# Two-layer transformer trunk on one core: dummy products in two waits, a moved pair of column products, and weight copies on other engines

## The chip, the core and the metric

The kernel runs on one core of a Trainium2 chip. The core's engines are TensorE (PE in the rows, its weight loads PEld), VectorE (DVE), ScalarE (ACT), GpSimd (POOL) and SyncE (SP), which issues the DMAs. They run side by side and wait for each other on semaphores. The metric is the device time of one execution in microseconds (us).

## The reference, cut to what matters

```python
D_MODEL, SEQ, DEPTH = 1024, 1024, 2
def reference(x, c, w_ada, b_ada, g_pre, g_post, w_in, w_out, diff_lambda, diff_subln):
    cond = jax.nn.silu(c)
    for i in range(DEPTH):
        ada = cond @ w_ada[i] + b_ada[i]
        shift, scale, gate = jnp.split(ada[:, None, :], 3, axis=-1)
        h = rms_norm(x, g_pre[i]) * (1.0 + scale) + shift
        u = h @ w_in[i]
        mix_in, z = u[..., :3 * BRANCH_WIDTH], u[..., 3 * BRANCH_WIDTH:]
        if i % N_MIXERS == 0:
            y = stick_breaking_attention(mix_in)
        else:
            j = i // N_MIXERS
            y = diff_attention(mix_in, diff_lambda[j], diff_subln[j], diff_lambda_init(i))
        y = (y * jax.nn.silu(z)) @ w_out[i]
        x = x + gate * rms_norm(y, g_post[i])
    return x
```

mix_in holds q, k and v for 16 heads of 64. Everything is float32.

## The kernel before, in words

**Arithmetic.** A float32 product is made from two reduced-precision parts of each operand: "high" is a rounded copy, "low" is the rest. One tile of 128 rows of the sum costs three products of 128x512: high with high, high weights with low activations, low weights with high activations. So every operand has a high copy (mostly ScalarE's) and a low subtraction (VectorE's or GpSimd's) before TensorE can use it.

**Stages.** The preparation (class `Prologue`) normalises x, turns it (feature rows on partitions), computes shift and scale, and projects q, k and v of the first pair of heads. Then layer 0 runs eight pairs of heads; in each the attention of the pair stands between the projection products of this pair's z (the gate branch) and the next pair's q, k and v (L666). The last pair has no next one, and takes the first part of the output projection (L1134) instead. `project_out` does the rest and, after layer 0, the first pair of layer 1. Layer 1 has the same shape with differential attention. Each engine has one written-out program; nothing is reordered at run time.

**The preparation on TensorE.** `warm(n)` multiplies a bf16 tile of zeros, which nothing reads; `turn(t)` turns one of eight row tiles; `row(n, h)` multiplies the conditioning vector with a slice of w_ada; `columns(i)` brings shift and scale, which lie in a row (i even) or are still to be summed over partitions (i odd), into columns, with eight tiny matmuls (L529). After `columns(0)` and `columns(1)` VectorE makes the first half of the columns, and then for each unit (128 features by 512 tokens) ScalarE writes h_hi (L346) and VectorE h_lo (L447). `project(kinds, phase, ...)` is the projection (L544): phase 0 is features 0 to 511 by tokens 0 to 511, phase 1 the same features by tokens 512 to 1023, phase 2 features 512 to 1023, which need `columns(2)` and `columns(3)`. The kinds are 0 (q), 1 (k) and 2 (v). VectorE sums `columns(1)`'s operand with L418 to L424.

**After it.** ScalarE copies the q and k sums out of PSUM (L686), packs them per head (L747: q and two copies of k for each of two heads), copies v, and makes the high part of z's weights (`split_hi(act, 0, 3)`, L632). These weights are loaded into the slot that k's weights leave. VectorE packs the low parts (L756 to L762) and GpSimd makes the low part of z's weights (L638). Head 0 of a pair is used in steps 0 to 7 of 16, head 1 from step 8 on.

**The last pair of layer 1.** In step 2 TensorE multiplies the first of four token tiles with the output weights, feature row by feature row: of the eight rows w_out is cut into it uses 0 to 6, each as soon as its high copy stands (`weights_ready`). ScalarE makes the copies of rows 0 to 5 (L983), VectorE those of 6 and 7 (L989), GpSimd all eight low parts (L1001). Then comes token tile 1, which needs its own high and low activations (ScalarE L1048, VectorE L1056) and the PSUM bank, which ScalarE empties (L1141).

Of the kernel before, what the change touches and what calls it, by code (L numbers as in the profile page):

```python
# [29 lines left out]
KT = D // P  # L30
# [156 lines left out]
class Prologue:  # L187
# [6 lines left out]
    T = ((0, 1), (6, 7), (0, 1), (6, 7), (6, 7), (4, 1), (6, 7), (4, 1))  # L194
    WARM = (24, 12)
    ACC = ((3, 4), (0, 1), (6, 7))
# [295 lines left out]
    def tensor(self, pe):  # L492
        nc, m = self.nc, self.m
# [69 lines left out]
        turn(3)  # L563
        columns(0)
        columns(1)
        pe.wait_ge(self.left_kept, 4)
        pe.wait_ge(self.right_kept, 4)
# [7 lines left out]
        project((0, 1), 1, range(self.LOW))  # L575
        for phase in range(2):
            project((2,), phase, range(self.LOW))
        columns(2)
        columns(3)
        project((0, 1), 2, range(self.LOW))  # L580
        for kind in range(3):
# [331 lines left out]
class OutProjection:  # L913
# [5 lines left out]
    def __init__(self, nc, m, sb, layer, order, sems, before=None):  # L919
# [19 lines left out]
        if before:  # L939
            self.gate_stored, self.weights_in = before.gate_stored, before.weights_in  # L940
            self.weights_hi_done, self.weights_lo_done = before.weights_hi_done, before.weights_lo_done
            self.weights_hi_second_done = before.weights_hi_second_done
            self.hi_done, self.lo_done, self.product, self.kept = (before.hi_done, before.lo_done, before.product,
                                                                   before.kept)
            self.early_hi, self.early_lo = before.early_hi, before.early_lo
            self.early_product, self.early_kept = before.early_product, before.early_kept
            return

        def sem(name):
            return nc.alloc_semaphore(f"o_{name}")  # L950
# [3 lines left out]
        self.weights_hi_done, self.weights_lo_done = sem("w_hi_done"), sem("w_lo_done")  # L954
        self.weights_hi_second_done = sem("w_hi_second_done")

# [28 lines left out]

    def weights_hi_second(self, dve, k):

        dve.wait_ge(self.weights_in[k // 2], 16 * self.layer + 16)
        self.nc.vector.tensor_copy(self.m["wo_hi"][:, k, :], self.m["wo_raw"][:, k, :]  # L989
                                   ).then_inc(self.weights_hi_second_done, 1)  # L990

    def weights_ready(self, engine, k):

        if self.layer and k >= 6:
            engine.wait_ge(self.weights_hi_second_done, k - 5)
        else:
            engine.wait_ge(self.weights_hi_done, KT * self.layer + k + 1)

# [13 lines left out]
    EARLY = 2 * (2 * HI + 2 * (HI + LO))  # L1012
# [164 lines left out]
def stick_breaking(nc, m, pro, proj, outp, w_out, w_ada, x, gate_rows):  # L1177
# [69 lines left out]
    HI_OWN, HI_NEXT = {0: (4, 5)}, {8: 0, 11: 1, 12: 2, 15: 3}  # L1247
# [31 lines left out]
    pack = HeadPacking(nc, m, "s")  # L1279
# [32 lines left out]
    with nc.Block() as block:  # L1312
# [163 lines left out]
        def _(act):  # L1476
# [51 lines left out]
            def pack_hi(p, n):  # L1528
                if n in (0, 1):
                    act.wait_ge(proj.u_done, done(6 * p + 2 * n + 1))  # L1530
                if n == 0:
                    act.wait_ge(logits, done(NCH * (p - 1) + LOOP.at[TILES // 2] - 1))
                if n == 3:
                    act.wait_ge(logits, done(NCH * p - 1))
                pack.hi(act, n)
# [6 lines left out]
            def pair(p, first, project):  # L1542
                for s in range(TILES if project else STEPS):
# [17 lines left out]
                    for kind, half in U_AT[s] if project else ():  # L1561
                        keep_u(p + 1, kind, half)
                    for n in () if first else HI_OWN.get(s, ()):
                        pack_hi(p, n)
# [10 lines left out]
            for kind in range(2):  # L1575
                for half in range(2):
                    keep_u(0, kind, half, m["pm"][pro.ACC[kind][half]])
                for n in ((0,), (1, 2, 3, 4, 5))[kind]:
                    pack_hi(0, n)
            for half in range(2):  # L1580
                keep_u(0, 2, half)
            proj.split_hi(act, 0, 3)
            pair(0, True, True)
# [6 lines left out]
        def _(dve):  # L1590
# [93 lines left out]
            def pair(p, first, project):  # L1684
                for s in range(TILES if project else STEPS):
# [12 lines left out]
                    lo_own = LO_OWN if project else LAST_LO_AT  # L1698
                    if not first and s in lo_own:
                        pack.lo(dve, p, lo_own[s])  # L1700
# [17 lines left out]

            for n in range(4):
                pack.lo(dve, 0, n)  # L1720
            pair(0, True, True)
            with dve.Fori(1, PAIRS - 1) as p:
# [5 lines left out]
        def _(pool):  # L1728
# [17 lines left out]

            proj.split_lo(pool, 0, 3)
            pair(0, True)
# [4 lines left out]
def differential(nc, m, pro, proj, outp, w_out, first, source, gate_rows):  # L1753
# [37 lines left out]
    LAST_Z_AT = [[0, 1] if s == EARLY - 1 else [] for s in range(STEPS)]  # L1791
    OUT_HI_AT = {1: (0, 1, 2), 2: (3, 4, 5)}
    OUT_LO_AT = {2 + k // 2: (k, k + 1) for k in range(0, KT, 2)}
# [32 lines left out]
    with nc.Block() as block:  # L1826
# [112 lines left out]
        def _(act):  # L1939
# [78 lines left out]
            def pair(p, project):  # L2018
                for s in range(STEPS):
# [32 lines left out]
                    for k in () if project else OUT_HI_AT.get(s, ()):  # L2052
                        outp.weights_hi(act, k)
                    if s == EARLY and not project:
                        outp.early_split_hi(act, EARLY_AT[s], pack)
                    for t, h in early_kept:
# [18 lines left out]
        def _(dve):  # L2075
# [91 lines left out]
            def pair(p, project):  # L2167
                for s in range(STEPS):
# [24 lines left out]
                    if s == EARLY + 1 and not project:  # L2193
                        z_gate(p)
                    if s == EARLY and not project:
                        for k in (6, 7):
                            outp.weights_hi_second(dve, k)
                    if s in EARLY_AT and (s == EARLY or s > EARLY + 1) and not project:
# [384 lines left out]
```

## Time and profile before

| | |
|---|---|
| median of 3 runs | 1428.17 us (1428.1 to 1428.66) |
| the profiled execution's own time | 1429.55 us |
| its span on the core | 1427.8 us |
| TensorE busy (matmul) | 1366.0 us, 96% |
| VectorE, ScalarE, GpSimd busy | 1012.6, 905.2, 384.4 us |
| mean granted TensorE clock | 0.985 of full speed |

The span is the part of the execution in which the engines work; about 1.8 us lie around it. A granted clock of 1.00 is the upper level (2.4 GHz) and 0.50 the lower one (1.2 GHz). TensorE's busy time counts a slow product as busy, so a stretch at 0.50 looks full.

### The profile page before, as it was taken

To read this page: it belongs to the slowest core of one execution; us is meant where nothing else is said; L and a number is where in the kernel's file an instruction comes from. 1 tells how busy PE (TensorE), PEld (TensorE's weight loads), DVE (VectorE), ACT (ScalarE), POOL (GpSimd) and SP (SyncE) were. 2 spreads that over 40 slices of the span, in tenths; PEclk is the share of its full clock that TensorE was granted. 3 is DMA by queue.
4 is the path that set the end of the run, shared out by engine and by line. 5 is a ranking of instruction groups with operands and counts; after the bars stand their busy time and mean duration, and the time that the engine had idled before them with its cause. 6 is when DMAs were issued, how large, how long until landed. Compare 5 with 4: busy or idle time off the path is not lost. (4 is left out here: it accounts for less than half of the span.)

```text
span 1427.8 us, 23466 instructions
## 1 busy us (share of the span) xinstructions
PE 1366.0 (96%) x7206; PEld 1127.8 (79%) x7206; DVE 1012.6 (71%) x1868; ACT 905.2 (63%) x1778; POOL 384.4 (27%) x255
## 2 busy tenths in 40 slices
PE   6979999999999999998899899999999999998997
PEld 3568888888888888877778688888888888886776
DVE  4556889787878787889578675757575656566654
ACT  3546667666666666676356576867676767675742
POOL 2103434333433343344100122222222222226000
PEclk8889999999999999999999999999999999999999
DMA  9111212031212121231143111010111111103114
GB/s 341 61 37 52 67 39 81 22 87 30 73 44 73 44 67 46 71 132 46 52 150 101 30 31 39 25 39 29 29 29 29 29 29 29 44 15 118 45 62 146
DMA packets 88591, 89.90 MB, mean 63 GB/s; under 512 B 3065, under 2 KB 68834, under 8 KB 88546
## 3 DMA queue, kind: packets, MB, share of 16 engines
q1 hardware_dynamic: 88256, 89.15, 19.8%
q8 instruction: 25, 0.41, 0.1%
q10 hardware_dynamic: 290, 0.18, 0.1%
q14 instruction: 20, 0.16, 0.0%
HBM read 80.92 MB, written 8.40 MB: 63 GB/s over the span
## 5 line engine op out<-in xcount | busy, mean ns | idle before, releaser
L666 PE MATMUL bank<-h_hi,w_hi 128*128 128x512 f32 x928 | 377.4, 407 | 4.9 <-POOL w_lo L638 4.9
L666 PE MATMUL bank<-h_hi,w_lo 128*128 128x512 f32 x928 | 373.6, 403 | 0.0
L666 PE MATMUL bank<-h_lo,w_hi 128*128 128x512 f32 x928 | 371.2, 400 | 0.0
L1739 POOL TENSOR_TENSOR sa<-sa,keep 128x128 f32<-128x128 f32 (+7 forms) x128 | 223.9, 1749 | 388.4 <-DVE keep L1601 388.4
L666 PEld LDWEIGHTS bank<-h_hi,w_hi 128*128 128x128 f32 x928 | 176.4, 190 | 33.8 <-issue 6.5
L1601 DVE TENSOR_TENSOR_SCAN keep<-keep 128x128 f32<-128x128 f32 (+7 forms) x128 | 194.8, 1522 | 10.9 <-ACT keep L1490 10.9
L666 PEld LDWEIGHTS bank<-h_hi,w_lo 128*128 128x128 f32 x928 | 175.8, 189 | 32.1
L666 PEld LDWEIGHTS bank<-h_lo,w_hi 128*128 128x128 f32 x928 | 176.0, 190 | 29.0
L638 POOL TENSOR_TENSOR w_lo<-w_raw,w_hi 128x1024 fp32r<-128x1024 f32 x30 | 72.6, 2419 | 431.0 <-ACT w_hi L632 431.0
L1489 ACT ACTIVATE sa<-bank 128x512 f32<-128x512 f32 (+2 forms) x192 | 94.6, 492 | 73.6 <-PE bank L1373 44.1
L1502 ACT ACTIVATE wt_hi<-bank 128x512 fp32r<-128x512 f32 (+2 forms) x192 | 87.5, 490 | 54.8 <-PE bank L1389 50.8
L1610 DVE TENSOR_TENSOR wt_lo<-bank,wt_hi 128x512 fp32r<-128x512 f32 (+2 forms) x192 | 100.5, 550 | 25.5 <-ACT wt_hi L1502 23.5
L2105 DVE CUSTOM_DVE_ANT_0 b<-bank,bias 128x512 f32<-128x512 f32 (+2 forms) x96 | 51.0, 557 | 70.0 <-PE bank L1855 69.7
L1951 ACT ACTIVATE b<-b,stat 128x128 f32<-128x128 f32 (+3 forms) x64 | 49.7, 776 | 72.7 <-DVE stat L2114 44.3
L1490 ACT ACTIVATE keep<-bank 128x512 f32<-128x512 f32 (+2 forms) x192 | 95.4, 497 | 0.0
L2141 DVE TENSOR_TENSOR wt_lo<-bank,wt_hi 128x512 fp32r<-128x512 f32 (+2 forms) x96 | 50.5, 554 | 58.2 <-ACT wt_hi L1974 57.2
L1389 PE MATMUL bank<-ident,sa 128*128 128x128 f32 x576 | 85.3, 275 | 0.3 <-DVE v L1681 0.3
L1959 ACT ACTIVATE b<-b,stat 128x128 f32<-128x128 f32 (+3 forms) x64 | 49.5, 773 | 45.9 <-DVE stat L2125 45.8
L1407 PE MATMUL bank<-wt_hi,v 128*128 128x256 f32 x320 | 75.8, 272 | 1.0 <-DVE wt_lo L1610 1.0
L1854 PE MATMUL bank<-k_hi,q 128*128 128x512 f32 (+2 forms) x192 | 70.2, 366 | 6.3 <-DVE stat L2105 4.5
L1407 PE MATMUL bank<-wt_lo,v 128*128 128x256 f32 x320 | 74.7, 280 | 0.0
L1389 PEld LDWEIGHTS bank<-ident,sa 128*128 128x128 f32 x576 | 66.0, 140 | 9.6 <-DVE v L1681 1.3
(253 smaller groups left out, 2919.5 us busy)
## 6 DMA issues: line engine op xcount, KB each, us to landing
w_raw<-in_w_in_dram SPq DMA_DIRECT2D x62, 512.0 KB, 4.1
ada_slice<-in_w_ada_dram SPq DMA_DIRECT2D x64, 256.0 KB, 2.7
p_ada<-in_w_ada_dram SPq DMA_DIRECT2D x8, 1024.0 KB, 13.0
wo_raw<-in_w_out_dram SPq DMA_DIRECT2D x8, 1024.0 KB, 4.8
p_x<-in_x_dram SPq DMA_DIRECT2D x8, 512.0 KB, 7.9
o_x<-in_x_dram SPq DMA_DIRECT2D x8, 512.0 KB, 4.1
x_between<-o_res SPq DMA_DIRECT2D x8, 512.0 KB, 2.9
o_x<-x_between SPq DMA_DIRECT2D x8, 512.0 KB, 4.7
```

What stands on the lines that cost most here:

```text
L638: engine.tensor_tensor(self.m["w_lo"][s][:, :, :], self.m["w_raw"][s][:, :, :], self.m["w_hi"][s][:, :, :].bitcast(F32), ALU.subtract).the ...
L666: mm = nc.tensor.matmul(self.bank[half][:, :], w[:, k, :], h[:, k, half * HALF:(half + 1) * HALF], start=(i == 0), stop=(i == GROUP - 1))
L1389: mm = nc.tensor.transpose(T[b % 2][:, j * P:(j + 1) * P], a[:, at:at + P], m["ident"][:, :])
L1407: mm = nc.tensor.matmul(O[:, c0:GW], m["v"][h][:, j, :], w[:, j, c0:GW], start=(j == 0 and w is m["wt_hi"]), stop=(j == tiles - 1 and w is ...
L1489: nc.scalar.activation(m["sa"][ring(t)][:, at:at + w], L[ch % 3][:, 0:w], ACT.Sigmoid, scale=SCALE)
L1490: nc.scalar.activation(m["keep"][KEEP[t]][:, at:at + w], L[ch % 3][:, 0:w], ACT.Sigmoid, scale=-SCALE).then_inc(gates, 1)
L1502: nc.scalar.activation(dst, T[b % 2][:, 0:w].rearrange("p (j q) -> p j q", q=P), ACT.Copy).then_inc(hi_done, 1)
L1601: nc.vector.tensor_tensor_scan(keep, keep, keep, 1.0, ALU.mult, ALU.bypass).then_inc(scanned, 1)
L1610: nc.vector.tensor_tensor(m["wt_lo"][:, js, c0:c0 + P], T[b % 2][:, 0:w].rearrange("p (j q) -> p j q", q=P), m["wt_hi"][:, js, c0:c0 + P]. ...
L1739: nc.gpsimd.tensor_tensor(a[:, at:S], a[:, at:S], m["keep"][KEEP[t]][:, at + 1:S + 1], ALU.mult).then_inc(weighted, 1)
L1854: nc.tensor.matmul(bank[:, 0:w], qs, m["k_hi"][n][:, k0:k0 + w], start=True, stop=False)
L2105: nc.vector.tensor_tensor_reduce(out=x[:, at:at + w], in0=L[ch % 3][:, 0:w], in1=m["bias"][:, at:at + w], scale=1.0, scalar=-3e38, op0=ALU ...
```

## The change

1. Two calls of `warm` (20 and 6 products on zeros) stand before and after `columns(1)`.
2. `columns(2)` and `columns(3)` stand between the two phases of v's projection, no longer behind them.
3. For the first pair, ScalarE makes the high part of z's weights ahead of v's two copies and of the two packs of head 1's k; these packs move into step 0 of the pair. VectorE packs head 1's low parts in steps 0 and 1, as in the other pairs, and makes the low part of z's weights in GpSimd's place.
4. In the last pair of layer 1 ScalarE makes the high copies of rows 6 and 7 of w_out too; the high activations of token tile 1 stand behind row 3 and ahead of row 4.

```diff
@@ -192,7 +192,7 @@
-    WARM = (24, 12)
+    WARM = (24, 12, 20, 6)
@@ -562,7 +562,9 @@
         turn(3)
         columns(0)
+        warm(self.WARM[2])
         columns(1)
+        warm(self.WARM[3])
         pe.wait_ge(self.left_kept, 4)
         pe.wait_ge(self.right_kept, 4)
         project((0, 1), 0, range(self.LOW))
@@ -573,10 +575,10 @@
         project((0, 1), 1, range(self.LOW))
-        for phase in range(2):
-            project((2,), phase, range(self.LOW))
+        project((2,), 0, range(self.LOW))
         columns(2)
         columns(3)
+        project((2,), 1, range(self.LOW))
         project((0, 1), 2, range(self.LOW))
         for kind in range(3):
             project((kind,), 2, range(0 if kind == 2 else self.LOW, KT))
...
@@ -983,18 +983,9 @@
-    def weights_hi_second(self, dve, k):
-
-        dve.wait_ge(self.weights_in[k // 2], 16 * self.layer + 16)
-        self.nc.vector.tensor_copy(self.m["wo_hi"][:, k, :], self.m["wo_raw"][:, k, :]
-                                   ).then_inc(self.weights_hi_second_done, 1)
-
     def weights_ready(self, engine, k):
 
-        if self.layer and k >= 6:
-            engine.wait_ge(self.weights_hi_second_done, k - 5)
-        else:
-            engine.wait_ge(self.weights_hi_done, KT * self.layer + k + 1)
+        engine.wait_ge(self.weights_hi_done, KT * self.layer + k + 1)
 
@@ -1560,7 +1551,7 @@
-                    for n in () if first else HI_OWN.get(s, ()):
+                    for n in HI_OWN.get(s, ()):
                         pack_hi(p, n)
@@ -1575,11 +1566,11 @@
-                for n in ((0,), (1, 2, 3, 4, 5))[kind]:
+                for n in ((0,), (1, 2, 3))[kind]:
                     pack_hi(0, n)
+            proj.split_hi(act, 0, 3)
             for half in range(2):
                 keep_u(0, 2, half)
-            proj.split_hi(act, 0, 3)
             pair(0, True, True)
@@ -1696,7 +1687,7 @@
-                    if not first and s in lo_own:
+                    if s in lo_own:
                         pack.lo(dve, p, lo_own[s])
@@ -1716,8 +1707,9 @@
-            for n in range(4):
+            for n in range(2):
                 pack.lo(dve, 0, n)
+            proj.split_lo(nc.vector, 0, 3)
             pair(0, True, True)
@@ -1744,7 +1736,6 @@
-            proj.split_lo(pool, 0, 3)
             pair(0, True)
@@ -1789,7 +1780,7 @@
-    OUT_HI_AT = {1: (0, 1, 2), 2: (3, 4, 5)}
+    OUT_HI_AT = {1: (0, 1, 2), 2: (3, 4, 5, 6, 7)}
     OUT_LO_AT = {2 + k // 2: (k, k + 1) for k in range(0, KT, 2)}
     EARLY_AT = {1: 0, 2: 1, 3: 2, 6: 3}
     MULTIPLY = shares(outp.EARLY, [0] * 2 + [28, 28, 14, 14, 14, 28, 14])
@@ -2051,8 +2042,8 @@
                     for k in () if project else OUT_HI_AT.get(s, ()):
                         outp.weights_hi(act, k)
-                    if s == EARLY and not project:
-                        outp.early_split_hi(act, EARLY_AT[s], pack)
+                        if k == 3:
+                            outp.early_split_hi(act, EARLY_AT[s], pack)
                     for t, h in early_kept:
                         if s != EARLY + 1 or h == 1:
                             outp.early_keep(act, t, h)
@@ -2192,9 +2183,6 @@
-                    if s == EARLY and not project:
-                        for k in (6, 7):
-                            outp.weights_hi_second(dve, k)
                     if s in EARLY_AT and (s == EARLY or s > EARLY + 1) and not project:
                         outp.early_split_lo(dve, EARLY_AT[s], pack)
```

TensorE in the preparation, from the fourth row tile to the first projection product:

```order
 L501 MATMUL bank<-ident,p_x_119 128x128 x8
 L529 MATMUL bank<-ones,p_ada_row 128x1 x4
+L507 MATMUL bank<-p_warm 128x512 x20
 L529 MATMUL bank<-ones,p_acc_125 128x1 x4
+L507 MATMUL bank<-p_warm 128x512 x6
 L544 MATMUL bank<-h_hi,w_hi_55 128x512
 L544 MATMUL bank<-h_lo,w_hi_55 128x512
```

Twenty dummy products now stand between the two column groups and six behind them.

TensorE further on, between v's phase 0 and phase 1 (`p_v_hi`, `p_v_lo` are v's weights):

```order
 L544 MATMUL bank<-h_lo,p_v_hi 128x512
 L544 MATMUL bank<-h_hi,p_v_lo 128x512
+L529 MATMUL bank<-ones,p_ada_row 128x1 x4
+L529 MATMUL bank<-ones,p_acc_127 128x1 x4
 L544 MATMUL bank<-h_hi,p_v_hi 128x512
 L544 MATMUL bank<-h_lo,p_v_hi 128x512
```

TensorE a little later, at the end of v's phase 1 and the start of phase 2 (q's weights):

```order
 L544 MATMUL bank<-h_lo,p_v_hi 128x512
 L544 MATMUL bank<-h_hi,p_v_lo 128x512
-L529 MATMUL bank<-ones,p_ada_row 128x1 x4
-L529 MATMUL bank<-ones,p_acc_127 128x1 x4
 L544 MATMUL bank<-h_hi,w_hi_55 128x512
 L544 MATMUL bank<-h_lo,w_hi_55 128x512
```

The eight column matmuls (4 and 4 in the program) moved ahead of v's second twelve products.

ScalarE from the end of the preparation to pair 0 (`w_hi_56<-w_raw_58` is z's weights, `k_hi_74` head 1's k), before:

```order
L686 ACTIVATE uq<-bank 128x512 x2
L747 ACTIVATE q_71<-uq 64x1024
L686 ACTIVATE uk<-bank 128x512 x2
L747 ACTIVATE k_hi_73<-uk 64x1024 x2
L747 ACTIVATE q_72<-uq 64x1024
L747 ACTIVATE k_hi_74<-uk 64x1024 x2
L686 ACTIVATE uv<-bank 128x512 x2
L632 ACTIVATE w_hi_56<-w_raw_58 128x1024
L1489 ACTIVATE sa_84<-bank 128x128
L1490 ACTIVATE keep_88<-bank 128x128
```

and now:

```order
L688 ACTIVATE uq<-bank 128x512 x2
L749 ACTIVATE q_71<-uq 64x1024
L688 ACTIVATE uk<-bank 128x512 x2
L749 ACTIVATE k_hi_73<-uk 64x1024 x2
L749 ACTIVATE q_72<-uq 64x1024
L634 ACTIVATE w_hi_56<-w_raw_58 128x1024
L688 ACTIVATE uv<-bank 128x512 x2
L1480 ACTIVATE sa_84<-bank 128x128
L1481 ACTIVATE keep_88<-bank 128x128
L749 ACTIVATE k_hi_74<-uk 64x1024 x2
```

The z copy stands two groups earlier, and the head 1 packs have gone behind the first sigmoids.

ScalarE in step 2 of the last pair of layer 1, before:

```order
L1974 ACTIVATE wt_hi<-bank 128x128
L983 ACTIVATE wo_hi<-wo_raw 128x1024 x3
L1048 ACTIVATE o_ahead_hi_164<-y 128x896
L1141 ACTIVATE o_parked_159<-bank 128x512 x2
L1048 ACTIVATE o_ahead_hi_163<-y 128x896
```

and now:

```order
L1965 ACTIVATE wt_hi<-bank 128x128
L983 ACTIVATE wo_hi<-wo_raw 128x1024
L1039 ACTIVATE o_ahead_hi_164<-y 128x896
L983 ACTIVATE wo_hi<-wo_raw 128x1024 x4
L1132 ACTIVATE o_parked_159<-bank 128x512 x2
L1039 ACTIVATE o_ahead_hi_163<-y 128x896
```

Two more weight copies stand ahead of the parked sums (`o_parked_159`), and the activations of token tile 1 (`o_ahead_hi_164`) ahead of four of the copies instead of behind them all.

## Rows read from the trace of the kernel before

**Rows 1.** the page of the profile, its first line
```profile
span 1427.8 us, 23466 instructions
```

**Rows 2.** who waited for whom, TensorE, whole span: total, times, longest
```profile
PE bank L1134 <- DVE o_ahead_lo L1056: 8.1, 4, 4.3
```

**Rows 3.** busy time by stretch: PE, PEld, DVE, ACT, POOL, clock, DMA
```profile
22.40:25.80 3.40, 2.00 (x16) 1.67 (x15) 2.42 (x5) 2.28 (x4) 0.32 (x1) 1.00 1.08 368
25.80:39.40 13.60, 4.92 (x15) 4.26 (x16) 10.95 (x17) 5.62 (x8) 7.99 (x8) 0.50 1.06 378
73.60:80.40 6.80, 6.05 (x14) 4.79 (x15) 6.63 (x12) 4.74 (x7) 0.00 (x0) 0.50 0.00 0
105.00:240.00 135.00, 135.00 (x762) 113.34 (x760) 108.23 (x142) 88.90 (x185) 49.79 (x29) 1.00 0.19 56
1309.20:1316.00 6.80, 6.18 (x15) 4.82 (x16) 3.69 (x7) 1.43 (x3) 6.80 (x3) 0.50 0.00 0
```

**Rows 4.** timeline of TensorE, preparation: start, length, instruction, idle before
```profile
24.50 1.05 PE L529 MATMUL bank<-ones,p_ada_row 1*128 1x1 f32 x8 [1.15 <-ACT p_ada_row L336]
31.90 1.87 PE L529 MATMUL bank<-ones,p_acc 128*128 128x1 f32 x8 [6.35 <-DVE p_acc L424]
36.34 0.77 PE L544 MATMUL bank<-h_hi,w_hi 128*128 128x512 f32 x1 [2.58 <-DVE h_lo L447]
...
50.69 8.21 PE L512 MATMUL bank<-p_ada,cond_act 128*1 128x512 f32 x16
```

**Rows 5.** timeline of the weight loads, dummy products at the start
```profile
5.41 3.12 PEld L507 LDWEIGHTS bank<-p_warm 128*128 128x128 bf16 x15 [0.17 <-issue]
```

**Rows 6.** timeline of TensorE, end of the preparation
```profile
70.91 1.05 PE L529 MATMUL bank<-ones,p_acc 128*128 128x1 f32 x8
74.35 0.77 PE L544 MATMUL bank<-h_hi,w_hi 128*128 128x512 f32 x1 [2.38 <-DVE h_lo L447]
...
88.19 0.39 PE L544 MATMUL bank<-h_hi,p_v_hi 128*128 128x512 f32 x1
...
93.40 0.39 PE L544 MATMUL bank<-h_hi,p_v_lo 128*128 128x512 f32 x1
...
98.89 0.77 PE L666 MATMUL bank<-h_hi,w_hi 128*128 128x512 f32 x1 [4.86 <-POOL w_lo L638]
```

**Rows 7.** timelines of DVE, ACT and POOL there; the page's issues (last)
```profile
73.51 0.69 DVE L447 TENSOR_TENSOR h_lo<-p_h,h_hi 128x512 fp32r<-128x512 f32 x1 [0.37 <-ACT h_hi L346]
...
81.80 0.69 DVE L447 TENSOR_TENSOR h_lo<-p_h,h_hi 128x512 fp32r<-128x512 f32 x1
...
112.98 1.20 DVE L638 TENSOR_TENSOR w_lo<-w_raw,w_hi 128x1024 fp32r<-128x1024 f32 x1
...
89.02 2.14 ACT L747 ACTIVATE k_hi<-uk 64x1024 fp32r<-64x1024 f32 x2
...
95.25 1.06 ACT L632 ACTIVATE w_hi<-w_raw 128x1024 fp32r<-128x1024 f32 x1
...
96.46 2.34 POOL L638 TENSOR_TENSOR w_lo<-w_raw,w_hi 128x1024 fp32r<-128x1024 f32 x1 [37.33 <-ACT w_hi L632]
...
w_raw<-in_w_in_dram SPq DMA_DIRECT2D x62, 512.0 KB, 4.1
```

**Rows 8.** timelines of DVE, ACT and PE, last pair of layer 1
```profile
1293.54 1.08 DVE L1056 TENSOR_TENSOR o_ahead_lo<-y,o_ahead_hi 128x896 fp32r<-128x896 f32 x1
...
1301.13 5.50 DVE L989 CAST wo_hi<-wo_raw 128x1024 fp32r<-128x1024 f32 x2
1306.55 3.22 DVE L1056 TENSOR_TENSOR o_ahead_lo<-y,o_ahead_hi 128x896 fp32r<-128x896 f32 x1
...
1321.71 1.28 DVE L2156 SCALAR_TENSOR_TENSOR y<-y,lam,z_sig 128x1024 f32<-128x1024 f32 x1 [2.43 <-ACT z_sig L2001]
...
1299.84 2.94 ACT L983 ACTIVATE wo_hi<-wo_raw 128x1024 fp32r<-128x1024 f32 x3
...
1309.82 0.80 PE L1134 MATMUL bank<-wo_hi,o_ahead_hi 128*128 128x512 f32 x1 [4.27 <-DVE o_ahead_lo L1056]
```

More of the change, by code:

```diff
@@ L941, in __init__ @@
             self.weights_hi_done, self.weights_lo_done = before.weights_hi_done, before.weights_lo_done
-            self.weights_hi_second_done = before.weights_hi_second_done
             self.hi_done, self.lo_done, self.product, self.kept = (before.hi_done, before.lo_done, before.product,
@@ L954, in __init__ @@
         self.weights_hi_done, self.weights_lo_done = sem("w_hi_done"), sem("w_lo_done")
-        self.weights_hi_second_done = sem("w_hi_second_done")
         self.hi_done, self.lo_done = sem("hi_done"), sem("lo_done")
```

## The prediction

> **What bounds the kernel now.** I read the page first: a span of 1427.8 us [rows 1], in which TensorE is busy 96%. Then the table of busy time by stretch, for how full that really is. From 105 to 240 us, pair 0 and most of pair 1, TensorE is busy 135.00 of 135.00 us at the full clock [rows 3]: it is the bound, and whatever reaches it earlier at 105 us is kept to the end. So the question is what happens in the few places where it waits or runs at the lower clock. The list of waits names the largest, o_ahead_lo (L1056), 8.1 us in 4 waits, the longest 4.3 us [rows 2]; the timeline shows that this one stands in the last pair of layer 1. The other large ones are in the preparation: 6.35 us before the summed columns, 2.58 us before the first projection product [rows 4], 2.38 us behind `columns(3)`, 4.86 us for z's weights [rows 6]. Last, the granted clock. It is 0.50 from 25.8 to 39.4, from 73.6 to 80.4 and from 1309.2 to 1316.0 us [rows 3], and each of the waits for h_lo, for z's weights and for o_ahead_lo is followed by products at low clock. Their price: from 74.35 us [rows 6] to 80.40 us there are 14 products [rows 3], 6.05 / 14 = 0.432 us each; between 88.19 and 93.40 us there are 23 steps of 5.21 / 23 = 0.2265 us [rows 6]. A product at low clock costs 0.205 us more.
>
> **Part 1, the dummy products.** Dummies at full clock go at 3.12 / 15, some 0.21 us each [rows 5]; at low clock they can't be faster than 0.43. `columns(0)` ends at 25.55 us [rows 4] and the clock falls at 25.8, so the twenty start low. Both ends: all low 8.6 us, to 34.2 us; all fast 4.2 us, to 29.8. The summed columns are ready at 31.9 us [rows 4]. I take about half low (at the start of the kernel dummies ran at the fast spacing), an end near 31.7 us, nothing lost. `columns(1)` then runs at full clock, as `columns(0)` did: 1.05 instead of 1.87 us [rows 4], **0.8 us**. The ScalarE and VectorE work behind it starts 0.8 us earlier, up to the row products at 50.69 us [rows 4]. If the six dummies keep the clock for the first projection (36.34 us), some 7 products save 1.4 us, but TensorE only comes sooner to row tiles 4 to 7, which ScalarE is still scaling. I take nothing for it. The row products themselves take 8.21 us for 16 [rows 4]; part of them ran at low clock, and wholly at full clock they would be shorter, which I take as 1 us, for the range alone.
>
> **Part 2, columns between the halves of v.** The gap of 2.38 us [rows 6] is the way from `columns(3)` through VectorE's column sums, ScalarE's h_hi and VectorE's h_lo. Twelve v products, 12 x 0.2265 = 2.7 us, now lie in it: **2.4 us** gone. No gap, so no low clock: 14 x 0.205 = **2.9 us**. Given back: h_lo comes at VectorE's pace, 73.51 to 81.80 us in seven steps [rows 7], 1.18 us a unit. Phase 2 takes 6 products (1.36 us) for each of the first four units, but only 3 (0.68 us) for the last four. First unit ready at t, last at t + 8.3; TensorE would be at unit 8 at t + 0.4 + 5.4 + 2.0 = t + 7.8. It waits **-0.5 us**. The move needs the row kept and the sum ready 2.7 us sooner; `columns(3)` waited for nothing before it [rows 6], so both were there with room.
>
> **Part 3, z's weights.** The end of v and the first score come 0.8 + 2.4 + 2.9 - 0.5 = 5.6 us earlier: TensorE is ready for z at 98.89 - 4.86 - 5.6 = 88.4 us. The load is issued when k's sums are done, 88.19 - 5.6 = 82.6 us, and lands 4.1 us later [rows 7], 86.7. ScalarE has by then done q, k and three of the head packs (1.07 us each, [rows 7]), about 86.4, so the high copy runs 86.8 to 87.9 (1.06 us). Before it stood behind two more packs and v's copies, at 95.25. VectorE takes 1.20 us where GpSimd took 2.34 [rows 7]: ready at 89.1. TensorE waits 0.7 us instead of 4.86: **4.2 us**. The clock stays up: twelve products were low after 98.89, 12 x 0.205 = **2.4 us**. The packs moved into step 0 (2.1 us of ScalarE) and VectorE's three operations of head 1 (under 1.3 us each) hide under steps 0 to 7; head 1 is not touched before step 8. Without that cover they would cost 2.1 us. What is late next is the load itself: with any gain ahead of it, the chain load, copy, subtraction moves along.
>
> **Part 4, last pair of layer 1.** VectorE's two casts take 5.50 us, then o_ahead_lo 3.22 us [rows 8], both while GpSimd makes wo_lo; alone o_ahead_lo takes 1.08 us, and a copy on ScalarE 2.94 / 3 = 0.98 us [rows 8]. Now, from 1299.84 us on [rows 8] at 0.98 us a copy and as much for the activations, ScalarE finishes row 3 at 1300.8, the activations at 1301.8 and rows 4 to 7 at 1302.8, 1303.8, 1304.7 and 1305.7. o_ahead_lo starts at 1301.9 and ends by 1305.1 even at 3.22 us. Row 4 comes 1.0 us later than before; behind row 6 stand four products of tile 0 and two of the score (6 x 0.2265 = 1.4 us), so TensorE gets to tile 1 at 1306.1 and waits for ScalarE to empty the bank, which I put at 1306.25. It starts tile 1 there instead of at 1309.82: **3.6 us**, and 14 products at full clock save 14 x 0.205 = **2.9 us**. Against it: VectorE's next work now falls under GpSimd's wo_lo copies, which go on to about 1317 us. The gating y operation (1.28 us at 1321.71, [rows 8]) is on the path to the next scores and would start near 1315.4. At the ratio of [rows 8], 3.22 to 1.08, it loses up to 1.3 us until GpSimd stops: **-1.2 us**. Sum 5.3 us. The Trainium skill has the rule (GPSIMD Engine Reference, Specifications): GpSimd's memory interfaces are shared with VectorE, and VectorE instructions with two SBUF inputs contend. It gives no factor; the trace agrees.
>
> **Sum.** 0.8 + 2.4 + 2.9 - 0.5 + 4.2 + 2.4 + 5.3 = 17.5 us. The profiled execution took 1429.55 us, 1.4 above the median, so 1412.1 there and 1410.7 beside the median. I say 1411.
>
> **The rivals.**
>
> *A, the columns bring the clock down.* From 22.4 to 25.8 us TensorE was busy 2.00 of 3.40 us, half of it tiny column products, and the clock fell right behind it [rows 3]. The same eight tiny products now lie in the middle of v. If it falls there, some 8 to 16 products run low, +1.6 to +3.3 us (at 0.205), of which 0.5 is the wait for h_lo anyway: near 1412.5. For it: that row. Against it: dense products on both sides. The Trainium skill (TensorE: Matmul & The Clock Gate, What's actually happening) says the clock drops after an idle spell; by that rule this rival would cost nothing. The row shows a fall without one, so I keep it.
>
> *B, the clock turns out kinder.* The row products at full clock (1.0 us), the low stretch in layer 0's last pair, behind a 2.7 us wait, missed (0.7 to 1.4 us): 1408.5 to 1409.5. The same page says the point of the change varies from run to run; the earlier times differ by only 0.56 us, so little of that shows here.
>
> *C, the last pair gives little.* The chain of score, bias, exponential, z gate after 1316 us is VectorE's and ScalarE's, not TensorE's. If all of it slows by 3.22 / 1.08 under GpSimd, or TensorE's wait there grows and the clock falls in it (14 x 0.205 = 2.9 us), the 5.3 us shrink to 0 to 2.4: 1413.5 to 1416.
>
> *D, z's load doesn't come sooner.* If it is held by other transfers, up to the 4.2 us are lost: 1415. The DMA queues are empty before it in this stretch, so this is unlikely.
>
> *E, slower: the dummies leave the clock low.* If products on zeros didn't hold it and the preparation and pair 0 ran low from 25.8 us on, each us of it would cost 0.47 us. To eat 17.5 us it must last 37 us beyond today's low stretches; the longest now is 13.6 us [rows 3]. From there on it decides, at 1429 and more.
>
> **How the numbers follow.** The forecast, 1409.5 to 1412, 0.40. A 0.20, B 0.15, C 0.18, D 0.04, E and the unforeseen 0.03. The range takes the forecast, A, B and most of C: 1407.5 to 1415.5. What a measurement can tell from no change is about 0.2%, 2.9 us. All cases but E lie beyond it: faster 0.96, same 0.02, slower 0.02.
>
> **What would show it.** In the timeline after: `columns(1)` at 1.05 us with no gap of 6 us before it but dummies; ScalarE's first row tile scaled 0.8 us earlier; phase 2 starting near 71.2 us at spacing 0.2265; z's first product near 89.1 us behind a wait under 1.5 us; clock 1.00 over 73.6 to 80.4 and at z's start. In the last pair, counted from the high copy of row 3: row 4 two ScalarE operations later, tile 1 starting 5.4 us after it instead of 9, and no low stretch. I would be wrong if pair 0 showed TensorE waits that it doesn't have now, or if steps 3 and 4 of the last pair had new waits on VectorE of more than 3 us.

## The result and the profile after

The changed kernel takes 1417.46 us (median of 4 executions, 1414.61 to 1419.73), the kernel before 1428.41 us in the same batch: ratio 0.9922, interval 0.9910 to 0.9934. Five more executions in a later batch give a median of 1416.54 us (1415.22 to 1420.56), ratio 0.992 (0.9907 to 0.9934). It is faster, by 11 to 11.5 us. The forecast was 17.4 us (1411), and the range ended at 1415.5 us.

The profiled execution took 1418.14 us. The page's first line, and the windows (columns as in [rows 3]):

```profile
span 1416.4 us, 23517 instructions
```
```profile
25.80:39.40 13.60, 11.83 (x49) 6.47 (x49) 11.56 (x18) 6.30 (x10) 8.04 (x8) 0.87 1.06 379
87.30:90.70 3.40, 1.01 (x5) 0.86 (x6) 2.22 (x3) 3.38 (x6) 0.45 (x1) 1.00 0.68 204
90.70:94.10 3.40, 3.40 (x10) 2.66 (x9) 0.65 (x1) 1.08 (x2) 0.93 (x1) 0.50 0.08 27
797.30:800.70 3.40, 1.53 (x8) 1.32 (x9) 1.76 (x5) 0.99 (x3) 0.00 (x0) 1.00 0.51 142
800.70:804.10 3.40, 3.40 (x11) 2.75 (x10) 0.00 (x0) 0.11 (x2) 0.00 (x0) 0.50 0.05 14
1309.30:1312.70 3.40, 1.46 (x12) 1.46 (x13) 3.29 (x14) 1.64 (x3) 0.00 (x0) 1.00 0.00 0
1312.70:1316.10 3.40, 3.40 (x11) 2.65 (x9) 1.56 (x5) 1.85 (x5) 0.00 (x0) 0.50 0.00 0
```

The long low stretch of the preparation has shrunk, the one at 73.6 us is gone. One at 636.8 us is the same as in the kernel before (647.0). Three more stand at 90.7, 800.7 and 1312.7 us, each right behind a stretch in which TensorE was busy 1.0 to 1.5 of 3.40 us.

TensorE in the preparation, to be laid beside [rows 4] and [rows 6]:

```profile
25.75 5.95 PE L507 MATMUL bank<-p_warm 128*128 128x512 bf16 x19 [0.16 <-issue]
31.94 1.05 PE L529 MATMUL bank<-ones,p_acc 128*128 128x1 f32 x8 [0.24 <-DVE p_acc L424]
...
35.84 0.47 PE L544 MATMUL bank<-h_hi,w_hi 128*128 128x512 f32 x1 [1.53 <-DVE h_lo L447]
...
43.19 1.09 PE L501 MATMUL bank<-ident,p_x 128*128 128x128 f32 x8 [1.63 <-ACT p_x L326]
...
49.72 7.03 PE L512 MATMUL bank<-p_ada,cond_act 128*1 128x512 f32 x16
...
77.81 0.47 PE L544 MATMUL bank<-h_hi,w_hi 128*128 128x512 f32 x1 [0.25 <-DVE h_lo L447]
...
86.75 0.22 PE L1363 MATMUL bank<-k_hi,q 128*128 128x128 f32 x1
...
89.69 0.47 PE L668 MATMUL bank<-h_hi,w_hi 128*128 128x512 f32 x1 [2.54 <-DVE w_lo L640]
```

The wait of 2.38 us behind `columns(3)` [rows 6] is gone; in its place TensorE waits 0.25 us for VectorE near the end of phase 2, at 77.81 us. The same product of z that stood at 98.89 us [rows 6] starts at 89.69, behind a wait of 2.54 us where 0.7 was forecast. What fed it, on ScalarE and VectorE, and the DMA queues from 84 to 88 us (queue, kind: packets, MB, share of the engines):

```profile
84.31 1.06 ACT L749 ACTIVATE q<-uq 64x1024 fp32r<-64x1024 f32 x1
87.28 1.06 ACT L634 ACTIVATE w_hi<-w_raw 128x1024 fp32r<-128x1024 f32 x1 [1.91 <-DMA w_raw<-in_w_in_dram]
...
88.37 1.22 DVE L640 TENSOR_TENSOR w_lo<-w_raw,w_hi 128x1024 fp32r<-128x1024 f32 x1 [3.20 <-ACT w_hi L634]
```
```profile
q1 hardware_dynamic: 562, 0.28, 23.4%
q8 instruction: 1, 0.02, 1.6%
```

ScalarE was free at 85.4 us and waited 1.91 us for the load. In the records 15 of the load's 16 completions have come by 85.5 us and the last at 87.26. There is one packet of queue 8, kind "instruction", 16384 bytes, from 85.21 to 86.20 us; while it runs the load starts no packet, and its last three start from 86.19 us on. The records don't say which DMA engine a packet ran on; that these three stood behind the large one on the same engine is inferred from these times.

The last pair of layer 1, to be laid beside [rows 8], ScalarE, VectorE, TensorE, GpSimd:

```profile
1291.87 1.04 ACT L983 ACTIVATE wo_hi<-wo_raw 128x1024 fp32r<-128x1024 f32 x1
1292.81 0.94 ACT L1039 ACTIVATE o_ahead_hi<-y 128x896 fp32r<-128x896 f32 x1
1293.65 3.89 ACT L983 ACTIVATE wo_hi<-wo_raw 128x1024 fp32r<-128x1024 f32 x4
...
1293.79 2.45 DVE L1047 TENSOR_TENSOR o_ahead_lo<-y,o_ahead_hi 128x896 fp32r<-128x896 f32 x1 [0.54 <-ACT o_ahead_hi L1039]
...
1307.14 3.05 DVE L2147 SCALAR_TENSOR_TENSOR y<-y,lam,z_sig 128x1024 f32<-128x1024 f32 x1 [2.30 <-ACT z_sig L1992]
...
1298.17 0.47 PE L1125 MATMUL bank<-wo_hi,o_ahead_hi 128*128 128x512 f32 x1
...
1311.24 0.33 PE L1845 MATMUL bank<-k_hi,q 128*128 128x128 f32 x1 [3.04 <-DVE stat L2096]
...
1288.02 21.09 POOL L992 TENSOR_TENSOR wo_lo<-wo_raw,wo_hi 128x1024 fp32r<-128x1024 f32 x8 [10.55 <-ACT wo_hi L983]
```

The order of the copies does what was forecast: token tile 1 starts without a wait, 5.3 us after row 3's copy ends. But z's gate on VectorE (L2147) takes 3.05 us under GpSimd's low copies, which run to 1309.1, where it took 1.28 in [rows 8]; TensorE waits 3.04 us for what follows it, and then comes the low stretch at 1312.7.

Last, two places that the forecast did not touch, both of the changed kernel: VectorE in layer 0's last pair, and TensorE at layer 1's first score.

```profile
635.05 0.75 DVE L1635 SCALAR_TENSOR_TENSOR ada_acc<-ada_slice,cond_act,ada_acc 128x512 f32<-128x512 f32 x1 [1.04 <-DMA ada_slice<-in_w_ada_dram]
```
```profile
799.17 0.32 PE L1845 MATMUL bank<-k_hi,q 128*128 128x128 f32 x1 [1.88 <-DVE q L886]
```

The kernel before waits 1.84 us at that score too, and there its clock stayed up.

The slice of w_ada at 635.05 us came late as z's load did: 15 of its 16 completions by 633.61 us, the last at 635.03, and a packet of queue 8 from 631.73 to 632.71. What it costs is seen in TensorE's wait for the o_ahead_lo behind it, here in the changed kernel and in the same kernel without part 1 (told below):

```profile
636.91 0.77 PE L1125 MATMUL bank<-wo_hi,o_ahead_hi 128*128 128x512 f32 x1 [3.29 <-DVE o_ahead_lo L1047]
...
633.73 0.47 PE L1123 MATMUL bank<-wo_hi,o_ahead_hi 128*128 128x512 f32 x1 [2.71 <-DVE o_ahead_lo L1045]
```

**Where the 11.4 us of the two profiled executions are**, from the starts of the same products in both traces (the sum of the columns is ready within 0.04 us in both, so the two can be laid over each other):

| place | forecast | seen |
|---|---|---|
| turn of token tile 4: 43.70 to 43.19 | 0.8 | 0.5 |
| to the end of the row products: 50.69 + 8.21 to 49.72 + 7.03 | 0 | 1.6 |
| to the first score: 93.63 to 86.75 | 4.8 | 4.7 |
| z's weights and the clock behind them, 6.88 to 10.12 | 6.6 | 3.2 |
| layer 0's last pair | 0 | -0.6 |
| layer 1's first score, the new low stretch | 0 | -1.65 |
| layer 1's last pair | 5.3 | 3.4 |

Small drifts between these places make up the rest.

### The profile page after: what moved, and what is told of

The parts are those of the page before. It is cut to its first block and busy times, and to the rows that moved or that the text cites. A ratio compares the mean times of both kernels' runs of the same rounds, so it can differ in the third digit from the quotient of the medians.

```text
span 1416.4 us, 23517 instructions
## 1 busy us (share of the span) xinstructions
PE 1365.8 (96%) x7231; PEld 1125.7 (79%) x7232; DVE 1008.6 (71%) x1867; ACT 907.4 (64%) x1780; POOL 382.8 (27%) x254
```

## The experiments

Every kernel was timed beside the kernel before (medians of 1427.8 to 1428.7 us). Executions of one kernel lie up to 5.3 us apart, so medians are compared with the changed kernel's nine executions, median 1416.8 us, and the traces by the starts of the same products. The first four each take one part out. Two theories were formed on the result. F puts the missing gain into fixed places: z's load late, z's gate slowed by GpSimd's copies, a low stretch more behind each. P says that every term holds and only the places of the clock's changes cost it.

**Part 1 out.**
```diff
-        warm(self.WARM[2])
         columns(1)
-        warm(self.WARM[3])
```


> The changed kernel without its 26 dummy products, all else as changed. Two theories of the missing 6 us (17.5 forecast, 11.4 seen in the traces). Theory F (fixed places): the terms of the record hold except at z's weights (the load landed 1.8 us late, the clock fell once more) and in the last pair (z gate slowed by GpSimd, clock fell), and the rest is where the clock happened to fall. Theory P (position only): all terms hold and only the position of the clock's changes cost 6 us. For this kernel both expect columns(1) at 1.87 us again (+0.8) and the row products at 8.2 instead of 7.0 us (+1.2): 2.0 us slower than the changed kernel, give or take one low stretch (1.6 us). If the record's 0.8 alone were right: +0.8.

Measured 1415.75 us (1413.31 to 1417.28), ratio 0.9913 (0.9899 to 0.9926): 1.0 us under the changed kernel, where both theories had it 2.0 us slower. Its trace, TensorE:

```profile
32.27 1.86 PE L529 MATMUL bank<-ones,p_acc 128*128 128x1 f32 x8 [6.34 <-DVE p_acc L424]
...
44.07 1.09 PE L501 MATMUL bank<-ident,p_x 128*128 128x128 f32 x8
...
50.60 7.03 PE L512 MATMUL bank<-p_ada,cond_act 128*1 128x512 f32 x16
...
88.81 0.47 PE L666 MATMUL bank<-h_hi,w_hi 128*128 128x512 f32 x1 [0.80 <-DVE w_lo L638]
```

From the sum to the turn of tile 4 it is 11.80 us, with dummies 11.25: they gain 0.55 us. (All eleven traces with the dummies but one have 11.25 to 11.27 us; the changed kernel's second has 11.75, its clock fell at 35.1 us.) There the next wait takes over, 1.63 us for ScalarE's p_x. The row products take 7.03 us here too, so the dummies did not buy that. And z's wait is 0.80 us: in this execution the packet of 16384 bytes ran only at 92.1 us, after the load.

The 0.55 us is taken back in layer 0's last pair, by the dummies themselves. There the packet of queue 8 starts 2.9 to 3.6 us after the slice of w_ada is issued in all eleven traces with the 26 dummies, holds the last completion back by 1.3 to 1.5 us, and VectorE waits 0.8 to 1.4 us. In the three traces without them (the kernel before, this one, and the one with all three mends without dummies, below) it starts 8.8 us after the issue, and nothing is late. Three pairs of traces differ in the dummies alone; TensorE loses 0.6, 0.2 and 0.5 us more in that pair of heads with them. At 0.2265 us each 26 products are 5.9 us, about as much as the packet moved (5.2 to 5.9): this estimate would fit a packet that comes after so many of TensorE's instructions, but no run tests that.

**Part 2 out.**
```diff
         project((2,), 0, range(self.LOW))
+        project((2,), 1, range(self.LOW))
         columns(2)
         columns(3)
-        project((2,), 1, range(self.LOW))
```


> The changed kernel with the two later column groups behind all of v's products again. Both theories: the gap of 2.4 us and 14 products at low clock (2.9 us) come back, the wait for h_lo of 0.5 us goes: +4.8 us against the changed kernel. If the tiny column products in the midst of v cost anything by themselves (they brought no low clock in the changed kernel's trace), it would be less.

Measured 1419.6 us (1418.43 to 1420.0), ratio 0.9937 (0.9923 to 0.995): 2.8 us slower than the changed kernel, not 4.8. The products at 79 us come 4.7 us later than in the changed kernel, as worked out, the wait for h_lo is back (2.4 us) and the clock is low from 71.0 to 77.8. From pair 0 on 1.3 us are left, as z's load was on time here (wait 0.8 us) and no low stretch followed.

**Part 3 out** (z's weights, the packs and VectorE's share as before).
```diff
-            proj.split_hi(act, 0, 3)
             for half in range(2):
                 keep_u(0, 2, half)
+            proj.split_hi(act, 0, 3)
```


> The changed kernel with z's weights split as before (high part behind all packs and v's copies, low part on GpSimd, head 1 packed ahead of pair 0). Theory F: the wait goes from 2.54 to about 4.9 us and 12 instead of 8 products run low: +2.3 + 0.8 = +3.1 us against the changed kernel. Theory P: the record's 4.2 + 2.4 = +6.6 us, less 1.6 for the low stretch that is there already: +5.0 us.

Measured 1421.28 us (1419.66 to 1422.49), ratio 0.9951 (0.9938 to 0.9965): 4.5 us slower, nearer to P's 5.0 than to F's 3.1. In the trace, TensorE waits 4.87 us for GpSimd's w_lo, and pair 0 runs 3.55 us later: what part 3 gave the changed kernel's profiled execution. Executions in which the load is on time gain more from part 3, so the medians don't decide between the two.

**Part 4 out** (copies of rows 6 and 7 on VectorE, o_ahead_hi in its old place).
```diff
-    OUT_HI_AT = {1: (0, 1, 2), 2: (3, 4, 5, 6, 7)}
+    OUT_HI_AT = {1: (0, 1, 2), 2: (3, 4, 5)}
```


> The changed kernel with rows 6 and 7 of w_out copied by VectorE again and the activations behind them. Theory F: the wait of 4.3 us and 14 low products come back, against the 3.0 us wait and the low stretch behind the z gate that go: +3.4 us against the changed kernel. Theory P: the record's +5.3 us.

Measured 1420.84 us (1418.34 to 1421.08), ratio 0.9939 (0.9926 to 0.9953): 4.0 us slower. TensorE waits 4.28 us for o_ahead_lo, the stretch behind it is low (1300.5 to 1307.3), and 3.35 us are lost in the last pair: the part's worth, not 5.3.

The next three each mend one of the losses.

**z's weights loaded early**, into a tile of their own, once the row products are done.
```diff
+            sp.wait_ge(pro.row_done, 2)
+            proj.early_load(sp, proj.early_raw)
```


> The changed kernel, but the first pair's z weights are loaded some 25 us earlier into memory that is free then, and split from there; nothing else differs. Theory F: the load was what is late, so the high copy starts right behind the packs (about 85.4 us), the low part is ready about 87.7, TensorE waits 0.6 instead of 2.54 us and the clock stays up: 2.0 + 1.6 = 3.5 us faster than the changed kernel. Theory P: another wait takes its place (ScalarE's queue), 0 to 1 us faster.

Measured 1415.96 us (1412.69 to 1417.21), ratio 0.9908 (0.9894 to 0.9921): 0.8 us faster, not 3.5. z's wait is 0.66 us, and no low stretch follows it. But this trace has one from 68.0 to 71.4 us, behind `columns(2)` and `columns(3)`, which costs 1.6 us: from 79 us to pair 0 it gains 3.5, net 1.95.

**GpSimd's last low copy behind z's gate.**
```diff
+                        if k == 7:
+                            pool.wait_ge(z_gated, done(PAIRS - 1))
```


> The changed kernel, but in the last pair of layer 1 GpSimd makes the low part of row 7 of w_out only after VectorE's z gate. Theory F: the z gate takes 1.28 instead of 3.05 us, TensorE's wait before the next score shrinks from 3.04 to about 1.3 us, and the low stretch behind it may go: 1.8 to 3.4 us faster than the changed kernel. Theory P, or if the path runs elsewhere: no difference; if the late low part is waited for, slower.

Measured 1412.71 us (1411.2 to 1414.48), ratio 0.989 (0.9875 to 0.9905). VectorE's gate, TensorE's wait and the copy on GpSimd:

```profile
1304.38 1.28 DVE L2147 SCALAR_TENSOR_TENSOR y<-y,lam,z_sig 128x1024 f32<-128x1024 f32 x1 [2.34 <-ACT z_sig L1992]
...
1306.72 0.33 PE L1845 MATMUL bank<-k_hi,q 128*128 128x128 f32 x1 [1.27 <-DVE stat L2096]
...
1305.74 2.37 POOL L992 TENSOR_TENSOR wo_lo<-wo_raw,wo_hi 128x1024 fp32r<-128x1024 f32 x1 [1.77 <-DVE y L2147]
```

The gate is back at 1.28 us, the wait at 1.27, there is no low stretch, and the last pair gains 3.05 us. That shows the loss of part 4 and that GpSimd's copy beside the gate causes it; the median is 4.1 us faster. The other 2.9 us of this trace come before pair 0, where z's load was on time.

**Eight dummy products ahead of layer 1's first turn.**
```diff
+            for _ in range(8):
+                nc.tensor.matmul(m["pm"][6][:, :], m["h_hi"][:, 0, 0:P], m["h_hi"][:, 0, 0:HALF], start=True, stop=True)
```


> The changed kernel with eight dummy products (on real data, into a bank that nothing reads) in TensorE's wait of 1.9 us ahead of layer 1's first score. In the changed kernel's trace the clock fell behind this wait, before it did not. If the 1.6 us are lost there: about 1.6 us faster in executions in which it falls, nothing in the others, and less spread between executions. If the dummies outlast the wait: up to 0.3 us slower.

Measured 1416.63 us (1416.28 to 1419.7), ratio 0.9921 (0.9907 to 0.9934). No low stretch at 800 us, and 3.25 us ahead of the changed kernel behind it; 1.4 us of that go in the last pair, where the low stretch behind the wait is 6.8 us long instead of 3.4. The median did not move. That these dummies keep the clock is likely and not shown: none of the four traces with them has a stretch near 800 us, but of the ten without them only five have one, with the same wait of 1.84 to 1.89 us in all ten.

**All three.**


> All three: z's load early, the last low copy behind the z gate, dummies ahead of layer 1's first score. Theory F: the sum, 5 to 8 us faster than the changed kernel, about 1411 us, which is what the record forecast. Theory P: at most 1 to 2 us faster.

Measured 1411.33 us (1410.79 to 1412.62), ratio 0.9881 (0.9866 to 0.9897), 5.5 us under the changed kernel. The only low stretches between 40 and 1400 us are at 67.4 (columns) and 634.0 us. Windows of this trace around the columns:

```profile
64.00:67.40 3.40, 3.40 (x24) 2.88 (x23) 0.00 (x0) 0.00 (x0) 0.00 (x0) 1.00 0.00 0
67.40:70.80 3.40, 3.40 (x10) 2.66 (x10) 2.84 (x8) 2.76 (x4) 0.00 (x0) 0.50 0.00 0
```

TensorE waits for nothing from 64.0 to 67.4 us, but 16 of its 24 products have one column each. That alone doesn't settle it: the kernel with the low copy behind the gate has the same row, and its clock stays up:

```profile
64.10:67.50 3.40, 3.40 (x24) 2.86 (x22) 0.01 (x1) 0.00 (x0) 0.00 (x0) 1.00 0.00 0
67.50:70.90 3.40, 3.40 (x16) 2.83 (x17) 2.76 (x7) 2.68 (x4) 0.00 (x0) 1.00 0.00 0
```

The last four ran in one batch.

**The changed kernel again.**


> The changed kernel itself once more, in one batch with the next three. Theory F (its executions differ by whether the last queue of z's load lands late, and by where the low clock falls): median 1415 to 1418 us, single executions from 1413.5 to 1420, and in its trace a wait for z's low weights of either 0.8 or 2.2 to 2.5 us; of the stretches of low clock at 68, 92, 800 and 1310 us not the same set as in the first trace. Rival (the set of stretches belongs to the program): wait 2.5 us, stretches at 90.7, 636.8, 800.7 and 1312.7 us as in the first trace, executions within 1 us of each other.

Measured 1416.54 us, as told at the start. The trace (execution of 1420.56 us) has a z wait of 2.17 us, and low stretches at 69.2, 93.1, 639.2, 803.1 and 1315.1 us: one more than the first trace, and the early one is 35.1 to 41.9 us. The instruction packet runs from 87.32 to 88.43 us; 15 completions of the load have come by 88.01, the last at 89.48.

**All three without the dummies of the preparation** (the edit of part 1 out).


> The best kernel so far (z's load early, low copies behind z's gate, eight dummy products at layer 1's first turn) without the 26 dummy products of the preparation. Theory of the record (they are worth 0.8 us, by columns(1) and the first q,k at full clock): 1412.1 us where the kernel with them has 1411.3; in the trace the group of 8 turns of token tile 4 starts 0.8 us later, and so does everything behind it. Rival (they buy nothing that reaches the end): 1411.3 or less.

Measured 1412.31 us (1409.9 to 1413.65), ratio 0.9895 (0.988 to 0.991). From the sum to the turn of tile 4 it is again 11.79 us instead of 11.25 (32.24 to 43.49 in the kernel with them). The medians, 1.0 us apart where the prediction's term is 0.8, are within what executions scatter. In the two traces pair 0 runs 0.65 us earlier without the dummies, as no low stretch stands at 67 us there, and 1.0 us earlier from layer 1 on.

**All three, columns apart.**
```diff
-        project((2,), 0, range(self.LOW))
+        project((2,), 0, range(2))
         columns(2)
+        project((2,), 0, range(2, self.LOW))
         columns(3)
```


> The best kernel so far with columns(2) moved up into the first half of v, six products ahead of columns(3), which stays where it is. Theory (the two groups of 1.05 us of one-column products side by side bring the clock down at 67 to 71 us in half of the executions, 1.6 us each time; apart they do not): no low clock there, 1410.5 us, executions within 1.5 us. Rival (it is the sum of the two that counts, or the wait of h's copies for rows): the stretch at 67 us stays and the time is 1411.3, or p_ada_row is not there yet and PE waits.

Measured 1410.5 us (1409.73 to 1412.46), ratio 0.9884 (0.9868 to 0.9899), the fastest kernel of this study: 17.6 us under the kernel before, 6 under the changed one. Windows around its columns:

```profile
63.60:67.00 3.40, 3.40 (x23) 2.87 (x22) 0.16 (x1) 0.00 (x0) 0.00 (x0) 1.00 0.00 0
67.00:70.40 3.40, 3.40 (x17) 2.83 (x17) 2.58 (x7) 2.50 (x4) 0.00 (x0) 1.00 0.00 0
```

Three of its four executions have a mean clock of 0.997, which none with the columns together reached (0.995 at best). But its first row, too, holds both groups (they start at 63.86 and 66.33 us, 16 products of one column), and in five of ten traces the clock stayed up with the groups together. One trace and four executions make it likely, not shown, that standing apart is what keeps the clock.

**Part 1 alone on the kernel before.**


> The kernel before with the 26 dummy products of the preparation alone (part 1). Theory of the record: low clock from 25.8 to 39.4 us shrinks to one stretch, columns(1) 1.05 instead of 1.87 us, turns of token tile 4 start 0.8 us earlier, 1427.5 us (ratio 0.9994). Rival (the work behind waits for something else, or the low clock at 50 us comes all the same): no difference. Rival on the other side (a fall of the clock lands elsewhere, in the row products or the first v): up to 1.6 us slower, 1430.

Measured 1428.2 us (1427.21 to 1429.79, 11 executions) beside 1428.06 (15): ratio 1.0004 (0.9995 to 1.0013). The mean clock rises from 0.986 to 0.989 and the time does not change. Its trace has the turn of tile 4 11.25 us after the sum, 7.03 us of row products, and then low stretches at 70.4, 94.3 and, which the trace of before lacks, 807.7 us.

## Why the prediction was wrong, by its steps

- **What bounds the kernel**: right. In pairs 0 to 6 the difference of the two traces stays within 0.2 us. All gains and losses lie where TensorE waits or its clock is low.
- **Part 1**, 0.8 us: `columns(1)` took 1.05 us as said, but only 0.55 us reach the turns, and layer 0's last pair takes 0.2 to 0.6 us back, where the dummies bring an instruction packet onto a load. Nothing that can be measured reaches the end. "I take nothing" for the first projection at full clock was right, for the reason given: the wait moved to p_x.
- **Part 2**, 4.8 us: right in every term. The traces give 2.4 us for the wait, 2.7 for the clock (2.9 forecast), and 0.25 us of wait for h_lo instead of 0.5; 4.7 in all.
- **Part 3**, 6.6 us: the step that failed first is "lands 4.1 us later ... TensorE waits 0.7 us". The wait was 2.54 us, and "the clock stays up" fell with it, eight products at low clock, 1.6 us. Order, copies and subtraction were right: where the load is on time the wait is 0.8 us. Of the seven traces with the high copy in its new place and the load in its old one, three (the changed kernel's two and part 4 out) have the instruction packet over its tail and wait 2.2 to 2.5 us; in the other four it runs elsewhere, and they wait 0.8. All four with the early load wait 0.66. Rival D had this, a load held by another transfer, and called it unlikely because the queues were empty ahead of the load: the packet comes from another queue, and while the load runs.
- **Part 4**, 5.3 us: the first half was right (tile 1 starts at 1298.17 us, 5.3 us after the high copy of row 3 ends, 5.4 forecast, at full clock). The step that failed is "-1.2 us": the gate's ratio was 3.05 / 1.28 = 2.4, 1.8 us, and the low stretch behind a longer TensorE wait, 1.6 us, was left to rival C. C had both mechanisms and priced them too high: 3.4 us are left, not 0 to 2.4.
- **Not in the sum**: the new low stretch at 800 us (-1.65), a slice of w_ada that came 1.04 us late in layer 0's last pair (-0.6, part 1's doing), and the row products and turn at full clock (+1.6). This last was rival B's term. Kernels that have the preparation as before up to this point (part 1 out, twice) show 7.03 us as well, so it belongs to the execution of the kernel before that was profiled and not to the change: luck, and without it the two traces would differ by 9.8 us.
- **Rival A** was under-rated. Of the ten traces in which `columns(2)` and `columns(3)` stand together between v's halves, five have the stretch at 67 to 70 us. The Trainium skill (TensorE: Matmul & The Clock Gate, What's actually happening) ties a fall to an idle spell; the row of 64.00 to 67.40 us shows one behind a stretch without any, and there the measurement decides. Why the clock stayed up in the other five is open.
- **The range**: "the earlier times differ by only 0.56 us, so little of that shows here" was drawn from three executions. Fifteen of the kernel before span 1426.6 to 1429.39 us, nine of the changed one 1414.61 to 1420.56. The positions of low stretches vary, a stretch costs 1.6 us, and the sum counted every removal and no arrival.

What stays open: why the instruction packet meets z's load in some executions and not in others, and whether the dummies bring it there too (it ran at 85.2 us in the changed kernel and at 92.1 without them, but at 96.0 with part 2 out and the dummies in); and what makes the clock fall at 800 us in the changed kernel's two traces and not in that of before, with waits of 1.88 and 1.84 us.

## What to carry to other kernels

Where TensorE is full almost everywhere, price each wait twice: its length, and about 1.6 us for the low stretch behind it with the share of executions that have it; a forecast that counts only stretches removed is too fast. A load that must land just in time needs room of a microsecond or two for packets of other queues; an early load bought it here. Dummy products are not free either: they are instructions, and 26 of them moved a packet of instructions onto a load some 600 us later. And when a chain moves earlier, look at what it now runs beside: one low copy put behind z's gate was worth about as much as the whole reordering of the last pair.

## What was not expected of the hardware

- One packet of 16384 bytes of kind "instruction" (0.9 to 1.4 us long) held one of sixteen completions of z's load back by 1.4 to 1.8 us in three executions, and one of w_ada's by 1.3 to 1.5 us in all eleven with the 26 dummies, and with it the consumer.
- A VectorE operation with two inputs of 128x1024 took 3.05 us beside GpSimd's subtractions and 1.28 alone; o_ahead_lo took 2.45 beside them (3.22 in the kernel before) and 1.08 alone.
- The granted clock fell at 67.4 us behind 3.40 us in which TensorE was never idle, 16 of the 24 products having one column, and stayed up behind the same in another kernel's trace. And it can rise on the mean with no gain: 0.986 to 0.989 with part 1 alone, at an unchanged time.
